# Attention stage of a hybrid decoder step: softplus beside value products, first scores beside the projection, and page scores ahead of the next head's scores

## The reference, cut to what matters

```python
def _stick_breaking(q, k, v, mask, bias):
    z = jnp.einsum('bthd,bshd->bhts', q.astype(f32), k.astype(f32)) * (DH_B ** -0.5) + bias.astype(f32)[None, :, None, None]
    log_stay = jnp.where(mask, jax.nn.log_sigmoid(-z), 0.0)
    after = lax.cumsum(log_stay, axis=3, reverse=True)
    after = jnp.concatenate([after[..., 1:], jnp.zeros_like(after[..., :1])], axis=-1)
    w = jnp.where(mask, jnp.exp(jax.nn.log_sigmoid(z) + after), 0.0)
    return jnp.einsum('bhts,bshd->bthd', w, v.astype(f32))
...
qa, ka, va, oa, li, lf, qb, kb, vb = _even_proj(xpn, w_in_even[e], b_gate_even[e])
hb = _sb_prompt(qb, kb, vb, valid, b_sb_even[e])
...
k_all = jnp.concatenate([k_past, kb.astype(k_past.dtype)], axis=1)
hb = _stick_breaking(qb, k_all, v_all, mask, b_sb_even[e])
mix_s = _even_out(ha, oa, hb, g_head_even[e], w_out_even[e], dt)
```

## Time and profile before

| what | us |
|---|---|
| median of 3 executions | 1841.87 (1837.36 to 1848.1) |
| profiled execution, its own time | 1839.33 |
| its span, first to last instruction | 1837.7 |
| last eviction of the projection starts | 267.80 |
| first step of the output projection (ACT, L882) starts | 596.95 |
| granted PE clock over the span, share of full | 0.941 |

### The profile page before, as it was taken

The page is one execution under the profiler, slowest core; times in us unless marked ns, Lnnn a source line. Parts: engine busy times, 40 slices in busy tenths (PEclk is TensorE's granted clock), DMA queues, the critical chain, the costliest instruction groups (busy, mean ns, idle before and its releaser), DMA issues.

```text
span 1837.7 us, 31417 instructions
## 1 busy us (share of the span) xinstructions
PE 1661.6 (90%) x12398; PEld 1475.3 (80%) x12398; DVE 889.3 (48%) x1510; ACT 591.6 (32%) x937; POOL 91.0 (5%) x168
## 2 busy tenths in 40 slices
PE   6899986786887999999999988998879999999996
PEld 6899982333333999999999978996669999999996
DVE  4545443335343384444444564675545644444445
ACT  4222222243232462222222543324225422222224
POOL 0000001112212000000000000000000000000000
PEclk9899997788888999999999989998889999999998
DMA  4221137678764222222222221123202122222221
GB/s 173 103 69 70 58 116 262 198 224 261 230 195 142 94 71 87 72 91 91 91 91 70 77 79 61 47 94 115 91 35 78 61 93 91 91 79 81 84 76 51
DMA packets 50519, 195.11 MB, mean 106 GB/s; under 512 B 7325, under 2 KB 9534, under 8 KB 36610
## 3 DMA queue, kind: packets, MB, share of 16 engines
q1 hardware_dynamic: 35938, 139.49, 22.1%
q0 software_dynamic: 14496, 54.41, 8.7%
HBM read 182.19 MB, written 11.68 MB: 105 GB/s over the span
## 4 chain that ended last, share of the span: by engine, by line
PE 83%; DVE 8%; ACT 3%; issue 3%; SPq 2%; DMA 1%; DVEq 0%; POOLq 0%; POOL 0%; ACTq 0%
PE ps L298 21%; PE ps L300 21%; PE ps L299 20%; PE ps L1265 2%; PE ps L1293 2%; PE ps L1438 1%; PE ps L1441 1%; ACT whi L290 1%; PE ps L1474 1%; DVE wlo L294 1%; SPq L1242 1%; PE ps L1396 1%; PE ps L1897 1%; PE ps L1444 1%; DVE sp L1429 1%
## 5 line engine op out<-in xcount | busy, mean ns | idle before, releaser
L298 PE MATMUL ps<-xhi,whi 128*128 128x280 f32 x2112 | 627.2, 297 | 30.2 <-DVE wlo L294 17.5
L300 PE MATMUL ps<-xhi,wlo 128*128 128x280 f32 x2112 | 620.7, 294 | 0.0
L299 PE MATMUL ps<-xlo,whi 128*128 128x280 f32 x2112 | 620.0, 294 | 0.2 <-issue 0.2
L298 PEld LDWEIGHTS ps<-xhi,whi 128*128 128x128 f32 x2112 | 403.2, 191 | 36.4 <-DVE wlo L294 19.4
L299 PEld LDWEIGHTS ps<-xlo,whi 128*128 128x128 f32 x2112 | 402.7, 191 | 1.0 <-issue 0.5
L300 PEld LDWEIGHTS ps<-xhi,wlo 128*128 128x128 f32 x2112 | 402.6, 191 | 0.0
L294 DVE TENSOR_TENSOR wlo<-raw,whi 128x2048 fp32r<-128x2048 f32 x98 | 224.6, 2292 | 212.8 <-ACT whi L290 212.3
L290 ACT ACTIVATE whi<-raw 128x2048 fp32r<-128x2048 f32 x98 | 187.3, 1912 | 421.0 <-PE ps L300 420.2
L298 PE MATMUL ps<-dhi,whi 128*128 128x280 f32 x1024 | 300.5, 293 | 5.1 <-DVE wlo L294 4.6
L300 PE MATMUL ps<-dhi,wlo 128*128 128x280 f32 x1024 | 300.2, 293 | 0.0
L299 PE MATMUL ps<-dlo,whi 128*128 128x280 f32 x1024 | 299.2, 292 | 0.0
(11 more groups left out here) (378 smaller groups left out, 1586.3 us busy)
## 6 DMA issues: line engine op xcount, KB each, us to landing
raw<-in_weights_dram SPq DMA_DIRECT2D x98, 1024.0 KB, 4.8
kbuf<-in_k_cache_dram SPq DMA_DIRECT2D x128, 256.0 KB, 3.1
vbuf<-in_v_cache_dram POOLq DMA_DIRECT2D x128, 256.0 KB, 3.5
s0b<-in_gla_in_dram POOLq DMA_DIRECT2D x4, 1024.0 KB, 5.4
out_dram<-s0b POOLq DMA_DIRECT2D x4, 1024.0 KB, 4.1
hT<-in_x_dram SPq DMA_DIRECT2D x2, 1120.0 KB, 8.3
out_dram<-pj POOLq DMA_DIRECT2D x2, 1120.0 KB, 7.0
hT<-in_x_dram POOLq DMA_DIRECT2D x2, 1120.0 KB, 7.5
```

The lines of the kernel that those rows point to most:

```text
L298: pe.matmul(out, whi[:, par, t, :], hi, start=first, stop=False)
L299: pe.matmul(out, whi[:, par, t, :], lo, start=False, stop=False)
L300: return pe.matmul(out, wlo[:, par, t, :], hi, start=False, stop=last)
```

## The change

Work moves into the last projection pair. PE now does there, between its products, the scores of the new tokens, the scores of prompt head 0 (into four other PSUM banks), the new tokens' suffix product and the transposes of the first values (`ahead_pe`); ACT and DVE do the steps that belong to them (`ahead_act`, `ahead_first_dve`, `ahead_dve`). Three of four groups of the first key pages are loaded during that pair, into other buffers; the fourth follows when the projection is done. The values' loads stand ahead of the store of keys and values to DRAM on POOL.

Inside a turn, `z` is no longer rewritten (L1430 is gone): the suffix triangle now includes the diagonal (`incl`). The sums over later key blocks are made with fewer product columns: DVE adds blocks first (`T_`), and PE multiplies the sums. The weights are written to `sp`, and the mask is an addition of a large negative number ahead of the exponential. The softplus waits for nothing but its scores; DVE's write of `sp` waits for the value products instead. The own-heads product of a turn moves behind the suffix products of the next turn. The loop now runs over turns u = 1 and 2; turn 0 is written out ahead of it.

```diff
-        kbuf = [at(f"kbuf{g}", (o_hi + GB, o_lo + GB, o_M, o_M + GB)[g], [P, PG, 4, P]) for g in range(4)]
-        vbuf = [at(f"vbuf{g}", o_V + g * GB, [P, PG, 4 * P]) for g in range(4)]
+        kbuf = [at(f"kbuf{g}", (o_hT, o_hT + GB, o_K2, o_hi + GB)[g], [P, PG, 4, P]) for g in range(4)]
+        vbuf = [at(f"vbuf{g}", o_M + g * GB, [P, PG, 4 * P]) for g in range(4)]
...
-                pair4_pe(pe, i, "even", lambda n: mlstm_pe(pe, i, n))
+                pair4_pe(pe, i, "even", lambda n: mlstm_pe(pe, i, n) if i - 2 < H_A else ahead_pe(pe, n))
...
         def psoft_act(act, i, u):
-            if u:
-                act.wait_ge(S["a_v"], i * 2 + u)
...
         def psp_dve(dve, i, j):
+            if j:
+                dve.wait_ge(S["a_v"], i * 2 + j)
             for n, (r, c) in enumerate(FULL):
                 dve.wait_ge(S["a_l"], i * 4 + (2 * j + n + 1))
                 own.link(dve.scalar_tensor_tensor(sp[r, c], z[r, c], 0.0, lz[r, c], ALU.max, ALU.add))
-                own.link(dve.scalar_tensor_tensor(z[r, c], z[r, c], 0.0, lz[r, c], ALU.min, ALU.subtract))
             diag_mask(dve, sp, sp[0:N_META, METAQ]).then_inc(S["a_sp"], 1)
+            dve.wait_ge(S["a_sp"], i * 2 + (j + 1))
+            blk = lambda k, q, n=1: sp[:, KOFF[k] + P * (q - k):KOFF[k] + P * (q - k + n)]
+            own.link(dve.tensor_tensor(T_[0], blk(2, 3), blk(3, 3), ALU.add))
+            dve.tensor_tensor(T_[1][:, P:2 * P], blk(1, 3), T_[0], ALU.add)
+            own.link(dve.tensor_tensor(T_[1][:, 0:P], blk(1, 2), blk(2, 2), ALU.add))
+            dve.tensor_tensor(T_[2][:, 0:P], blk(0, 1), blk(1, 1), ALU.add)
+            dve.tensor_tensor(T_[2][:, P:3 * P], blk(0, 2, 2), T_[1], ALU.add).then_inc(S["a_T"], 1)
...
         def load_keys(sp_):
+            sp_.wait_ge(S["m_mix"], H_A)
+            sp_.wait_ge(S["mout"], 64)
+            for g in range(3):
+                load_k(sp_, 0, 0, g)
+            sp_.wait_ge(S["done"], DONE["out0"])
+            load_k(sp_, 0, 0, 3)
...
+        def ahead_pe(pe, n):
+            if n == 0:
+                new_scores_pe(pe)
+            elif n == 1:
+                pz_pe(pe, 0, 0, 4)
+            elif n == 3:
+                new_suffix_pe(pe)
+            elif n == 5:
+                values_pe(pe, 0, 0)
...
         def attn_pe(pe):
+            new_turn_pe(pe)
+            suffixes_pe(pe, 0, 0)
+            new_values_pe(pe)
+            pz_pe(pe, 0, 1)
+            qk_pe(pe, 0, 0)
+            pv_prompt_pe(pe, 0, 0)
+            tr_pe(pe, 0, 0)
+            suffix_pe(pe, 0, 0)
+            qk_pe(pe, 0, 1)
+            tr_pe(pe, 0, 1)
+            pv_pe(pe, 0, 0)
             def step(i, u, last):
                 suffixes_pe(pe, i, u)
+                own_out_pe(pe, i, u - 1)
                 suffix_pe(pe, i, u)
                 if not last:
                     qk_pe(pe, i, u + 1)
                     pz_pe(pe, i, u + 1)
+                if u == 2:
+                    values_pe(pe, i, u)
                 pv_prompt_pe(pe, i, u)
                 if not last:
                     tr_pe(pe, i, u + 1)
                 pv_pe(pe, i, u)
-                own_out_pe(pe, i, u)
...
+            pool.wait_ge(S["cld"], 16 * N_CONST)
+            load_values(pool)
             pool.wait_ge(S["ev"], EV["even"] + 56)
             for b in range(2):
                 pool.dma_start(kv_out[:, 4 * b:4 * b + 4, :], pj[:, KBB + 4 * b:KBB + 4 * b + 4, :]).then_inc(S["out"], 16)
-            pool.wait_ge(S["cld"], 16 * N_CONST)
-            load_values(pool)
```

More of the change, by code:

```diff
@@ L1442, in suffixes_pe @@
-            pe.matmul(ps[0:N_META, 3, 0:SEQ], after[0:N_META, 0:N_META], sp[0:N_META, META], start=True, stop=False)
-            for l in range(4):
-                pe.matmul(ps[0:N_META, 3, P * l:SEQ], ones[:, 0:N_META], sp[:, KOFF[l]:KOFF[l] + WID[l]],
-                          start=False, stop=l == 3)
-            pe.matmul(ps[0:N_META, 1, 384:400], after[0:N_META, 0:N_META], sp[0:N_META, METAQ], start=True, stop=True)\
-              .then_inc(S["a_A"], 1)
+                if k == 1:
+                    pe.matmul(ps[0:N_META, 1, 384:400], incl[0:N_META, 0:N_META], sp[0:N_META, METAQ], start=True, stop=True)
@@ new lines, in suffixes_pe @@
+                pe.matmul(ps[:, b, c:c + WID[k]], incl[:, :], sp[:, KOFF[k]:KOFF[k] + WID[k]], start=True, stop=k == 3)
+            pe.matmul(ps[0:N_META, 3, 0:SEQ], incl[0:N_META, 0:N_META], sp[0:N_META, META], start=True, stop=False)
+            pe.wait_ge(S["a_T"], i * 2 + (j + 1))
+            pe.matmul(ps[:, 2, P:2 * P], ones, sp[:, KOFF[3]:KOFF[3] + P], start=False, stop=True)
+            pe.matmul(ps[:, 1, P:2 * P], ones, sp[:, KOFF[2]:KOFF[2] + P], start=False, stop=False)
+            pe.matmul(ps[:, 1, 2 * P:3 * P], ones, T_[0], start=False, stop=True)
@@ L1489, in turns @@
                     own.start(i, own_steps)
-                for u in range(2):
+                for u in (1, 2):
                     step(i, u, False)
@@ L1493, in turns @@
                     own.end(3)
-            for u in range(2):
-                step(3, u, u == 1)
+            step(3, 1, True)
         def load_keys(sp_):
+            sp_.wait_ge(S["m_mix"], H_A)
[4 more added lines that the diff above has]
+            load_k(sp_, 0, 0, 3)
             for g in range(4):
-                load_k(sp_, 0, 0, g)
+                load_k(sp_, 0, 1, g)
             def step(i, u, last):
@@ L1503, in step @@
                     load_k(sp_, i, u + 1, g)
-            turns(sp_, step)
+            later_turns(sp_, step)
         def load_values(pool):
+            pool.wait_ge(S["done"], DONE["out0"])
             with pool.Fori(0, DEC_B // 2) as i:
@@ L1522, in step @@
                 pv_pe(pe, i, u)
-                own_out_pe(pe, i, u)
-                if u == 1 and not last:
-                    values_pe(pe, i, u + 1)
-            pz_pe(pe, 0, 0)
-            values_pe(pe, 0, 0)
-            qk_pe(pe, 0, 0)
-            tr_pe(pe, 0, 0)
-            turns(pe, step)
-        def attn_act(act):
+            later_turns(pe, step)
+            own_out_pe(pe, 3, 1)
+        def attn_act(act):
+            pexp_act(act, 0, 0)
+            act.wait_ge(S["mout"], 80)
+            pz_act(act, 0, 1)
+            page_z_act(act, 0, 0)
+            page_act(act, 0, 0)
+            psoft_act(act, 0, 1)
+            page_exp(act, 0, 0)
+            psoft_meta_act(act, 0, 1)
+            page_z_act(act, 0, 1)
+            page_act(act, 0, 1)
             def step(i, u, last):
@@ L2119, in _ @@
             even_pe(pe)
-            new_pe(pe)
             attn_pe(pe)
```

282 lines of the change are left out of this document (177 added, 105 removed).

## The result

The changed kernel takes 1782.93 us in the median of four executions (1777.87 to 1791.20), the kernel before 1842.11 (1837.36 to 1848.10): a ratio of 0.968, 95% interval 0.964 to 0.973, 59 us less. I had forecast 1765 with a range of 1752 to 1786. The sign and the range hold; the forecast itself is 18 us too low, and the time lies nearest to the 1780 of rival (a).

A forecast was written before the change was run, and what follows sets the result against it. PE's 46.9 us of waits for DVE's `sp` bound the attention; afterwards value loads set 28.1 us a turn. Second value products at 347 plus six loops and the end give 522.8 against 596.95, 74 us less: 1765 us, range 1752 to 1786.

The forecast's parts named there:

- rival (a): Value turns: clock or loads take the full price, 30.6 us a turn, 59 us less, 1780 us; chance 0.18.
- the split at 522.8: End of the attention: first output split at 522.8 where before had 596.95, 74 us less.
- transfers at the end: Key/value store and residual reload queue behind the last value loads; the output split covers them, else 5 us at most.
- Projection: Last projection pair takes on added PE and DVE work and ends near 277 instead of 268.
- Start: First turns: next key loads take 20.3 us; suffix products of turn 1 at 322, second value products at 347.
- Value loop: Value-page loads set the turn at 27.6 us: 4.86 to first load, 18.75 of issues, 4.7 landing, 0.7 between starts.
- Clock: PE's lower clock behind waits costs between 0 and 3.0 us a turn; 0.5 taken, giving 28.1 us a turn.
- Head loop: One head's suffix products to the next head's, through PE, ACT and DVE: 26.3 us with hand-overs.
- PE's work of 23.3 us: PE's own products in one turn after the change sum to 23.3 us, the floor of a turn.
- Covers: Steps costed at nothing, such as subtraction, mask, exponential, block sums and page softplus, finish before PE asks.
- Rival (c): Attention loop: an unseen wait keeps 35.2 us a turn, only the start is gained, 1808 us; chance 0.05.
- Rival (d): POOL's value-load issues get slower, by denser DVE work: at 2.2 us steps turns take 42 us, 1861; chance 0.04.

The follow-up runs named there:

- e2: Changed kernel with the first key products directly behind the first suffix products, ahead of new-token value products and the scores of head 1; 1775.68 us.
- e1: Changed kernel with a second buffer for one of the four value groups, used by odd turns; 1778.68 us.
- e6: Changed kernel loading only half of each key page (128 of 256 KB) from turn 2 on; 1779.88 us in one run.
- e9: Changed kernel with a turn's sixteen page numbers read into registers ahead of the buffer wait, instead of one before each load; 1758.97 us.
- e5: Changed kernel with ACT's softplus of the next head again waiting for this head's value products; 1808.77 us.
- e10: Changed kernel with page numbers read ahead, first key products early, and next head's scores ahead of next key products, one buffer set each; 1748.62 us.
- e4: Changed kernel with the projection part undone and the loop part kept, three first key groups still loaded during the projection; 1803.03 us.
- e11: Changed kernel with the softplus wait put back and four unread 512-column products filling PE's gap in every turn but the last; 1784.83 us.
- e8: Changed kernel with second value buffer, early first key products, and next head's scores and their softplus ahead of key products and page-score copy; 1760.80 us.

## Why the prediction was right, and where it was not

The sum by its own steps: I had the split at 522.8, it came at 540.57. Of these 17.8 us, 9.1 were lost by the second value products (356.09 against 347), 7.1 in the six loops behind them (356.09 to 531.87 is 29.3 a turn against 28.1), 1.6 at the end, where the last value products run mostly at the lower clock (5.23 us for 26, granted 0.69).

That the time lies in the range is in part luck. The range ends at rival (a) with 5 us for transfers at the end; nothing was lost to these, and 9.1 us were lost at the start, where no rival had put anything. (a) has the second value products at 347 and 30.6 us a turn, measured are 356.09 and 29.3: its 1780 comes near because the two differences nearly cancel.

- **Projection: right.** The end near 277: the last eviction starts at 276.41, the first suffix products at 277.34.
- **Start: the mechanism right, three terms too small.** Key loads do set it (e2). The rest of K(1)'s products, behind three waits of PE, ran almost wholly at the lower clock (6.48 us for 26, granted 0.55; I had put 317 for either clock, and they ended at 320.8), K(2) landed 22.5 us behind the products instead of 20.3, as its last load took 5.33 us beside the value loads of the next turn, and its 26 products took 5.63 us where I had 2.8. Together 8.8 of the 9.1 us.
- **Value loop: right that it binds, by e1, e6 and e9; its issues right to 0.1 us** (448.41 to 467.19 is 18.78, predicted 18.75). The landing is the term that was too small: 5.77, where I had taken the larger of two values of before, 4.7. The key loads were over when the last value loads of before went out; now they start 6.1 us ahead of the last one, where I had put some 4, and e6 shows that their bytes lengthen the landing: 4.1 us with half of them. I had carried a duration over from a trace whose traffic stood otherwise. The last turn, with no key loads beside it, has another term that I did not have: its last page landed after 3.83 us, but its second load started 3.77 us behind the first instead of 1.23, for a cause that stays open, and its loop took 30.05 us.
- **Clock: the mechanism of rival (a) is there, at half its price.** I chose 0.5 us a turn between 0 and 3.0. In the two late turns that wait, the value products take 5.32 us, and the buffers come free 1.4 to 1.7 us later than at full clock (5.51 and 5.78 against 4.09); spread over the four late turns that is 0.8 us a turn. The price of 3.0 was read too high: I compared with products in mid-turn, 2.8 us, but 26 products behind a wait take 3.62 at full clock (e6).
- **Head loop: right.** 26.3 us forecast; without the value loads it is 26.5 in e1 and e9, and 27 to 28.8 in turns with value transposes, where PE waits 1.06 us for `vP`, which I had left out. What I had not seen is how near the two loops lie and what the nearness means: lengthen the head loop by 2.5 us (e5) and the wait changes its place, to one where the clock falls.
- **PE's work of 23.3 us: right** for the turns without value transposes: e10 has such turns of 23.7, with PE busy for 23.6.
- **Covers: they held inside the turns.** In turn 0 PE waited 5.1 us for the pages' softplus on DVE (L1312), which I had covered only for later turns; the keys that it needs next landed later still, at 314.31. Otherwise no wait of PE for `a_T` or for prompt weights of more than 2.1 us in all, none for POOL's stores; the reload of the residual (12.4 us to landing) has nobody waiting for it.
- **Rival (c)** fell: the late turns last 29.0 us, not 35.2. The softplus wait is worth 15 us of the stage (e5) and the projection part 20 us of the total (e4); the fewer product columns and the moved own-heads product were not undone by themselves, so what each is worth stays open. **Rival (d)** fell: in the late turns value loads stood 1.22 to 1.33 us apart, with DVE busy 16.25 of 29.5 us. The rule of the Trainium skill (SBUF — State Buffer, Who interferes with whom) is not seen at work here; what spaces the loads is the read of the page number with its address steps, as e9 shows.

## What to carry to other kernels

When a wait is taken out of a turn, list every loop that passes through the turn, with issue, landing and products each, and give the landing as it will be beside the traffic of the new order; two loops within 3 us of each other are one risk. Look at the issuing queue first: sixteen loads in a row cost here twice their issue, because each had its own register load behind the wait, and moving these ahead of the wait was worth as much as more memory, until two queues' loads went out together and filled the DMA engines. A wait on TensorE can cost more than its length if it stands ahead of a long run of products, so that useless products in the gap can pay.

## What the runs showed that I had not expected

The clock lost behind one and the same wait has no fixed size. In e5 a wait of 3.84 us in front of the same products left one turn at a mean granted clock of 0.95 and the next at 0.77, 8.4 us longer.

The head steps of the second layer's linear attention, the same code in all kernels, have two lengths: each step holds the same wait of PE for DVE (3.64 us, 4.65 in the last), and a run of steps keeps either the higher mean clock or the lower one. The rows of one step, of the changed kernel and of e1:

```profile
1247.30:1270.80 23.50, 19.86 (x87) 14.31 (x86) 13.34 (x29) 6.78 (x17) 1.08 (x3) 0.85 0.24 90
```

```profile
1234.90:1262.00 27.10, 23.46 (x87) 16.34 (x86) 13.33 (x29) 6.78 (x17) 1.06 (x2) 0.75 0.21 80
```

DVE's busy time is the same to 0.01 us. The stretch behind the split, the same code in all kernels, thus lasted from 1236.8 us (e11) to 1249.7 (e8), a difference as large as several of the effects measured here, which is why the stages were compared by their marks.
